# Neighbourhood attention: two heads at a time on halves of TensorE's array, with the division by the row sums on GpSimd

## The chip, the core and the metric

One core of a Trainium2 chip runs the whole program, a hybrid network of two blocks in fp32 for one sequence of 512 positions. The metric is the device time of one execution in microseconds; the time before is the median of three runs.

## What is computed

The change touches one phase, the neighbourhood attention of the second block. The 512 queries lie on a grid of 8 rows and 64 columns. There are 8 heads of width 64. Every query attends, in one softmax, to the 512 positions of the grid and to 256 context keys. The window covers all 8 rows and 16 columns around the query; outside it the logits are minus infinity, and inside it a learned bias is added. Cut to what matters:

```
s_lat = einsum('bqhd,brkhd->bhqrk', q * 64 ** -0.5, k) + bias     # -inf outside the window of columns
s_ctx = einsum('bqhd,bchd->bhqc', q * 64 ** -0.5, kc)
p = softmax(concatenate([s_lat, s_ctx], -1), -1)                  # 512 + 256 logits a query
y = einsum('bhqrk,brkhd->bqhd', p_lat, v) + einsum('bhqc,bchd->bqhd', p_ctx, vc)
```

## The kernel before, in words

The program is a list of phases (`plan`, line 234; run by `run_plan`, line 239); each phase is a block in which every engine has its own queue of instructions, and all engines meet at its end. `attention_phase` (line 1647) stands between the second block's large projection (`project_phase`, line 325, whose products are lines 402 and 406) and the phases of the gated delta rule, which begin with a clearing of the used semaphores on GpSimd (`recycle`, line 197) and two loads (line 230).

On chip a tensor lies in planes of 128 partitions by 512 fp32 columns (`pl`). Queries and keys are stored transposed: plane `h // 2` holds heads 2i and 2i+1, one on partitions 0 to 63 and one on 64 to 127. A unit of work is one head `h` and one tile `i` of 128 queries, 32 units in all, head by head. For a unit n:

- SyncE loads the bias plus mask for the tile, 128 x 512, in two loads (line 1670) into one of three buffers `B`, once the unit three before has used its own.
- TensorE makes the scores (`scores`, lines 1681 and 1682): 64 contraction rows, so half of the array's rows, 128 x 512 to one PSUM bank and 128 x 256 (context) to another; banks 0 to 3 serve two units.
- VectorE (`logits`) scales the context part (line 1720), scales and adds the bias on the grid part (line 1721), both to the buffer `Sx` (three of them), takes the row maximum (line 1723) and negates it (line 1724).
- ScalarE (`exps`, line 1747) takes the exponential in place with the negated maximum as bias, and the row sum as accumulator.
- VectorE takes the reciprocal of the sum (line 1731) and multiplies the 128 x 768 row of `Sx` by it, in place (line 1732).
- TensorE transposes six blocks of 128 x 128 (line 1708) to banks 4 and 5. It waits for the copies of the unit before.
- ScalarE copies them to `PT` in two parts, 512 columns (line 1755) and 256 (line 1756).
- TensorE multiplies the values (`values`, line 1693): six products of 128 contraction rows and 64 output partitions, so half of the array's columns, added up in bank 6 or 7 on the half of the partitions that the head has.
- ScalarE stores 64 x 128 (`store`, line 1740).

The order on each engine is written out by hand. TensorE: the scores of unit n+2, the values of n-1, the transposes of n. VectorE: reciprocal and division of n, the logits of n+2. ScalarE: the copies of n, the store of n-1, the exponential of n+2. An fp32 product stands in the profile as two instructions, each with its load of weights: 64 where the code calls 32 times. A transpose is one.

Other lines that are named below: 2341, the experts' products, which write two experts to the two column halves by turns; 1145, products on quarters of the array in an earlier phase; 2454, a GpSimd `tensor_scalar` with a per-partition scalar on 128 x 1024; 1402 and 1984, GpSimd `tensor_tensor`; 1546, a VectorE reduction; 2016, a VectorE `tensor_scalar` from and to SBUF; 2010, a VectorE operation with one input in PSUM.

## Time and profile before

| | |
|---|---|
| runs | 3935.38, 3941.82, 3942.22 us; median 3941.82 |
| profiled execution | 3941.83 us, span 3940.0 us |
| busy share of the span | TensorE 88%, its loads of weights 48%, VectorE 32%, ScalarE 15%, GpSimd 16% |
| mean granted TensorE clock | 0.935 of full speed |
| the attention phase | 2590.9 to 2722.3 us of the span |

The span is the stretch between the first and the last instruction of the profiled execution; the execution's own time is what is compared with the runs. "PE" is TensorE's products, "PEld" its loads of weights, DVE VectorE, ACT ScalarE, POOL GpSimd and SP SyncE, the queue of loads. The granted clock is a share of 2.4 GHz: 0.50 is 1.2 GHz. A duration of a TensorE instruction includes its way through the array, so successive ones overlap; the cost of one in a stream is the distance between starts. Lines such as "x12" are instructions that follow each other and are shown as one.

### The profile page before, as it was taken

To read this page: it belongs to the slowest core of one execution; us is meant where nothing else is said; L and a number is where in the kernel's file an instruction comes from. 1 tells how busy PE (TensorE), PEld (TensorE's weight loads), DVE (VectorE), ACT (ScalarE), POOL (GpSimd) and SP (SyncE) were. 2 spreads that over 40 slices of the span, in tenths; PEclk is the share of its full clock that TensorE was granted. 3 is DMA by queue.
4 is the path that set the end of the run, shared out by engine and by line. 5 is a ranking of instruction groups with operands and counts; after the bars stand their busy time and mean duration, and the time that the engine had idled before them with its cause. 6 is when DMAs were issued, how large, how long until landed. Compare 5 with 4: busy or idle time off the path is not lost. (4 is left out here: it accounts for less than half of the span.)

```text
span 3940.0 us, 43660 instructions
## 1 busy us (share of the span) xinstructions
PE 3474.0 (88%) x18392; PEld 1885.3 (48%) x18392; DVE 1252.8 (32%) x2117; ACT 580.7 (15%) x1082; POOL 613.6 (16%) x400
## 2 busy tenths in 40 slices
PE   8988999989998899879999869998678785988886
PEld 3454444743444776334444434874477753422222
DVE  1442151032123664114440142145555543101112
ACT  1032030000003331000000010034132301100001
POOL 0000020000002452009968000000131300000000
PEclk9999999998998999989999879998789896999999
DMA  3211223201320000424434112221000011399995
GB/s 143 76 33 43 70 79 101 75 28 48 106 70 1 3 3 29 139 68 124 133 120 155 51 38 75 89 68 38 1 1 1 1 44 69 135 409 409 409 409 227
DMA packets 120513, 406.22 MB, mean 103 GB/s; under 512 B 13824, under 2 KB 18560, under 8 KB 120064
## 3 DMA queue, kind: packets, MB, share of 16 engines
q1 hardware_dynamic: 113408, 378.25, 27.1%
q0 software_dynamic: 6912, 25.17, 2.0%
q8 instruction: 148, 2.42, 0.3%
q14 instruction: 45, 0.37, 0.0%
HBM read 399.17 MB, written 4.19 MB: 102 GB/s over the span
## 5 line engine op out<-in xcount | busy, mean ns | idle before, releaser
L406 PE MATMUL ps<-arena 128*128 128x512 f32 (+1 forms) x3936 | 1679.3, 589 | 88.2 <-PEq L557 22.1
L406 PEld LDWEIGHTS ps<-arena 128*128 128x128 f32 x3936 | 757.1, 193 | 1010.4 <-issue 991.9
L2341 PE MATMUL ps<-arena 128*64 128x512 f32 x1024 | 244.9, 601 | 33.0 <-DMA arena<-in_w_gate 15.5
L1936 PE MATMUL ps<-arena 128*128 128x128 f32 x1312 | 174.9, 295 | 25.9 <-POOL arena L1991 25.9
L1402 POOL TENSOR_TENSOR arena<-arena 128x512 f32<-128x512 f32 x64 | 80.2, 1269 | 751.9 <-DVE arena L1504 658.5
L455 DVE SCALAR_TENSOR_TENSOR arena<-ps,params,arena 128x511 f32<-128x511 f32 (+4 forms) x266 | 190.7, 717 | 9.5
L2454 POOL TENSOR_SCALAR arena<-arena,small 128x1024 f32<-128x1024 f32 x64 | 183.3, 2864 | 8.1 <-DMA arena<-in_w_mod 4.2
L1936 PEld LDWEIGHTS ps<-arena 128*128 128x128 f32 x1312 | 168.5, 207 | 30.2 <-issue 16.8
L449 DVE TENSOR_SCALAR arena<-ps,params 128x512 f32<-128x512 f32 x68 | 55.1, 810 | 388.2 <-PE ps L406 388.2
L2341 PEld LDWEIGHTS ps<-arena 128*64 128x64 f32 x1024 | 71.0, 136 | 201.2 <-issue 198.2
L2407 DVE SCALAR_TENSOR_TENSOR arena<-ps,mods,arena 128x512 f32<-128x512 f32 x64 | 48.1, 751 | 371.6 <-PE ps L2329 370.8
L402 PE MATMUL ps<-arena 128*128 128x128 f32 (+1 forms) x1120 | 137.4, 284 | 15.8 <-PEq L557 15.8
L402 PEld LDWEIGHTS ps<-arena 128*128 128x128 f32 x1120 | 137.6, 207 | 18.1 <-issue 18.0
L1984 POOL TENSOR_TENSOR arena<-arena,cst 128x512 f32<-128x512 f32 x24 | 26.9, 1144 | 757.9 <-ACT arena L1968 757.9
L2369 PE MATMUL ps<-arena 128*64 128x512 f32 x512 | 121.5, 617 | 21.8 <-DMA arena<-in_w_down 12.4
L435 ACT ACTIVATE arena<-arena 128x512 f32<-128x512 f32 (+2 forms) x60 | 36.1, 601 | 688.7 <-DVEq L459 688.7
L2456 POOL TENSOR_TENSOR arena<-arena 128x1024 f32<-128x1024 f32 x56 | 132.1, 2359 | 4.7
L426 ACT ACTIVATE arena<-ps 128x512 f32<-128x512 f32 (+1 forms) x75 | 43.1, 574 | 597.0 <-PE ps L406 505.7
L304 PE MATMUL ps<-arena 128*128 128x512 f32 x256 | 116.7, 607 | 6.1 <-ACT arena L313 4.2
L1153 PE MATMUL ps<-arena 64*64 64x64 f32 x3072 | 114.6, 226 | 2.5 <-ACT arena L1342 2.5
L1153 PEld LDWEIGHTS ps<-arena 64*64 64x64 f32 x3072 | 104.6, 139 | 10.2 <-issue 6.4
L1976 ACT ACTIVATE arena<-ps 128x512 f32<-128x512 f32 x132 | 78.9, 597 | 183.0 <-PE ps L1936 124.9
(387 smaller groups left out, 3350.3 us busy)
## 6 DMA issues: line engine op xcount, KB each, us to landing
arena<-in_w_in SPq DMA_DIRECT2D x166, 512.0 KB, 3.6
arena<-in_w_gate SPq DMA_DIRECT2D x128, 512.0 KB, 15.5
arena<-in_w_up SPq DMA_DIRECT2D x128, 512.0 KB, 15.6
arena<-in_w_down SPq DMA_DIRECT2D x128, 512.0 KB, 15.6
arena<-in_w_mod POOLq DMA_DIRECT2D x48, 512.0 KB, 4.1
arena<-in_ffn_up SPq DMA_DIRECT2D x44, 512.0 KB, 3.6
arena<-in_w_branch SPq DMA_DIRECT2D x32, 512.0 KB, 3.6
arena<-in_w_out SPq DMA_DIRECT2D x16, 512.0 KB, 3.6
```

The lines of the kernel that those rows point to most:

```text
L304: ins = k.nc.tensor.matmul(k.bank(self.banks[i % len(self.banks)]), w[:, q * P:(q + 1) * P], self.fills[i][1](q), start=(q == 0), stop=(q ...
L402: last = nc.tensor.matmul(out[:, t * m:(t + 1) * m], j["rhs"](ka + q)[:, t * P:(t + 1) * P], w[:, q * m:(q + 1) * m], start=(q == 0), stop ...
L406: last = nc.tensor.matmul(out[0:m, 0:j["n"]], w[:, q * m:(q + 1) * m], j["rhs"](ka + q), start=(ka + q == 0), stop=(ka + q == kt - 1))
L455: ins = nc.vector.scalar_tensor_tensor(out=o, in0=s, scalar=c, in1=o, op0=ALU.mult, op1=ALU.add)
L1153: ins = nc.tensor.matmul(k.bank(b)[half(q), cell(h, i)], l[half(q), cell(h, i)], other, start=True, stop=True)
L1402: tt = lambda o, x, y, op: nc.gpsimd.tensor_tensor(o, x, y, op)
L1936: mm = lambda l, r: nc.tensor.matmul(out, l, r, start=True, stop=True)
L1976: nc.scalar.activation(dst, k.bank(n % BANKS), ACT.Copy).then_inc(act_out, 1)
L2341: ins = nc.tensor.matmul(k.bank(b + f)[64 * e:64 * e + 64, :], xev(q, 2 * p + e), slot(g + e)[:, f * 512:f * 512 + 512], start=(q == 0), s ...
L2369: ins = nc.tensor.matmul(k.bank(6 + f)[64 * e:64 * e + 64, :], HT(u)[:, q * P + 64 * e:q * P + 64 * e + 64], slot(g + e)[:, f * 512:f * 51 ...
L2454: k.pool_chain(pool, nc.gpsimd.tensor_scalar(o, w(m), c, None, ALU.mult))
L2456: k.pool_chain(pool, nc.gpsimd.tensor_tensor(a, a, o, ALU.add))
```

## The change

Two heads of a pair, 2i and 2i+1, are worked on together for each tile: `n` now counts pairs (16), `m` single heads (32), in the order tile by tile within a pair of heads. The scores of both heads are issued together, the grid parts of the two row halves to banks 0 and 1, then the context parts to banks 2 and 3; TensorE waits with them until the logits of the pair before have been taken. The values of both heads are issued by turns to the two halves of the partitions of bank 7, and stored with one operation of 128 x 128. The transposes of a head go to bank 6 (two blocks) and to bank 4 or 5 (four blocks); a head's transposes wait until ScalarE has copied the two blocks of the head before and the four blocks of the head two before. The division is now GpSimd's. The reduction writes the negated maximum itself. `Sx` has six buffers, `PT` and `B` four; the main part of the work space and a second one change places. The order: TensorE scores n+2, transposes 2n, transposes 2n+1, values n-1; VectorE logits of pair n+1, reciprocal 2n, maxima of pair n+1, reciprocal 2n+1; ScalarE exponential m+2, copies m (256 columns first, then 512), and after an odd m the store of the pair before. The call passes a second work space.

```diff
-def attention_phase(k, q, kt, v, kc, vc, y, w):
+def attention_phase(k, q, kt, v, kc, vc, y, w, w2):
     nc = k.nc
     pl = k.pl
     NK = T + CTX
-    units = [(h, i) for h in range(8) for i in range(TT)]
-    B = lambda n: pl(w + n % 3)
-    Sx = lambda n: pl(w + 3, 5)[:, (n % 3) * NK:(n % 3) * NK + NK]
-    PT = lambda n: pl(w + 8, 3)[:, (n % 2) * NK:(n % 2) * NK + NK]
-    cols = k.small
-    b_in = [k.sem(f"a_b_in{i}") for i in range(3)]
-    s_ok, s_used, max_ok, e_ok, p_ok, t_ok, t_out, y_ok, y_out = (k.sem(f"a_{s}") for s in ("s_ok", "s_used", "max_ok", "e_ok", "p_ok", "t_ok", "t_out", "y_ok", "y_out"))
+    heads = [(2 * hp + e, i) for hp in range(4) for i in range(TT) for e in range(2)]
+    UNITS = len(heads) // 2
+    B = lambda m: pl(w + m % 4 if m % 4 < 3 else w2 + 6)
+    Sx = lambda m: pl(w + 3, 9)[:, (m % 6) * NK:(m % 6) * NK + NK]
+    PT = lambda m: pl(w2, 6)[:, (m % 4) * NK:(m % 4) * NK + NK]
+    top = lambda m: k.small[:, 2 * (m % 6):2 * (m % 6) + 1]
+    total = lambda m: k.small[:, 2 * (m % 6) + 1:2 * (m % 6) + 2]
+    lat = lambda m: k.bank(m % 2)
+    ctx = lambda m: k.bank(2 + m % 2)[:, 0:CTX]
+    four = lambda m: k.bank(4 + m % 2)
+    two = k.bank(6)[:, 0:2 * P]
+    out = k.bank(7)[:, 0:P]
+    b_in = [k.sem(f"a_b_in{i}") for i in range(4)]
+    s_ok, s_used, max_ok, e_ok, r_ok, p_ok, t_ok, two_out, four_out, y_ok, y_out = (
+        k.sem(f"a_{s}") for s in ("s_ok", "s_used", "max_ok", "e_ok", "r_ok", "p_ok", "t_ok", "two_out", "four_out", "y_ok", "y_out"))
     with nc.Block() as block:
         @block.sync
         def _(sp):
-            for n, (h, i) in enumerate(units):
-                if n >= 3:
-                    sp.wait_ge(s_used, n - 2)
+            for m, (h, i) in enumerate(heads):
+                if m >= 4:
+                    sp.wait_ge(s_used, m - 3)
                 for r in range(2):
                     row = 2 * i + r
-                    sp.dma_start(B(n)[64 * r:64 * r + 64, :], k.dram["rpb"][h, :, (7 - row) * 64:(15 - row) * 64]).then_inc(b_in[n % 3], 16)
+                    sp.dma_start(B(m)[64 * r:64 * r + 64, :], k.dram["rpb"][h, :, (7 - row) * 64:(15 - row) * 64]).then_inc(b_in[m % 4], 16)
         @block.tensor
         def _(pe):
             def scores(n):
-                h, i = units[n]
-                lo = 64 * (h % 2)
-                if n >= 2:
-                    pe.wait_ge(s_used, n - 1)
-                a, b = k.bank(2 * (n % 2)), k.bank(2 * (n % 2) + 1)[:, 0:CTX]
-                lhs = pl(q + h // 2)[lo:lo + 64, i * P:(i + 1) * P]
-                nc.tensor.matmul(a, lhs, pl(kt + h // 2)[lo:lo + 64, :], start=True, stop=True)
-                nc.tensor.matmul(b, lhs, kc[lo:lo + 64, h // 2, :], start=True, stop=True).then_inc(s_ok, 1)
+                if n >= 1:
+                    pe.wait_ge(s_used, 2 * n)
+                hp, i = heads[2 * n][0] // 2, heads[2 * n][1]
+                lhs = lambda e: pl(q + hp)[64 * e:64 * e + 64, i * P:(i + 1) * P]
+                for e in range(2):
+                    nc.tensor.matmul(lat(2 * n + e), lhs(e), pl(kt + hp)[64 * e:64 * e + 64, :], start=True, stop=True)
+                for e in range(2):
+                    ins = nc.tensor.matmul(ctx(2 * n + e), lhs(e), kc[64 * e:64 * e + 64, hp, :], start=True, stop=True)
+                ins.then_inc(s_ok, 1)
+            def turn(m):
+                pe.wait_ge(p_ok, m + 1)
+                if m >= 1:
+                    pe.wait_ge(two_out, m)
+                if m >= 2:
+                    pe.wait_ge(four_out, m - 1)
+                for j in range(6):
+                    dst = two[:, j * P:(j + 1) * P] if j < 2 else four(m)[:, (j - 2) * P:(j - 1) * P]
+                    ins = nc.tensor.transpose(dst, Sx(m)[:, j * P:(j + 1) * P], k.const("ident"))
+                ins.then_inc(t_ok, 1)
             def values(n):
-                h, i = units[n]
-                lo = 64 * (h % 2)
-                pe.wait_ge(t_out, n + 1)
-                if n >= 2:
-                    pe.wait_ge(y_out, n - 1)
-                out = k.bank(6 + n % 2)[lo:lo + 64, 0:P]
+                hp = heads[2 * n][0] // 2
+                pe.wait_ge(four_out, 2 * n + 2)
+                if n >= 1:
+                    pe.wait_ge(y_out, n)
                 for j in range(6):
-                    vv = v[:, j, h * 64:h * 64 + 64] if j < 4 else vc[:, j - 4, h * 64:h * 64 + 64]
-                    ins = nc.tensor.matmul(out, vv, PT(n)[:, j * P:(j + 1) * P], start=(j == 0), stop=(j == 5))
+                    for e in range(2):
+                        c = (2 * hp + e) * 64
+                        vv = v[:, j, c:c + 64] if j < 4 else vc[:, j - 4, c:c + 64]
+                        ins = nc.tensor.matmul(out[64 * e:64 * e + 64, :], vv, PT(2 * n + e)[:, j * P:(j + 1) * P], start=(j == 0), stop=(j == 5),
+                                               skip_group_check=True)
                 ins.then_inc(y_ok, 1)
             scores(0)
             scores(1)
-            for n in range(len(units) + 1):
-                if n + 2 < len(units):
+            for n in range(UNITS):
+                if n + 2 < UNITS:
                     scores(n + 2)
+                turn(2 * n)
+                turn(2 * n + 1)
                 if n >= 1:
                     values(n - 1)
-                if n < len(units):
-                    pe.wait_ge(p_ok, n + 1)
-                    if n >= 1:
-                        pe.wait_ge(t_out, n)
-                    for j in range(6):
-                        ins = nc.tensor.transpose(k.bank(4 + j // 4)[:, (j % 4) * P:(j % 4 + 1) * P], Sx(n)[:, j * P:(j + 1) * P], k.const("ident"))
-                    ins.then_inc(t_ok, 1)
+            values(UNITS - 1)
         @block.vector
         def _(dve):
             link = lambda ins: k.dve_chain(dve, ins)
             def logits(n):
-                dve.wait_ge(s_ok, n + 1)
-                dve.wait_ge(b_in[n % 3], 32 * (n // 3 + 1))
-                if n >= 3:
-                    dve.wait_ge(t_ok, n - 2)
-                nc.vector.tensor_scalar(Sx(n)[:, T:NK], k.bank(2 * (n % 2) + 1)[:, 0:CTX], 0.125, None, ALU.mult)
-                nc.vector.scalar_tensor_tensor(out=Sx(n)[:, 0:T], in0=k.bank(2 * (n % 2)), scalar=0.125, in1=B(n), op0=ALU.mult, op1=ALU.add).then_inc(s_used, 1)
-                dve.wait_ge(s_used, n + 1)
-                link(nc.vector.tensor_reduce(cols[:, 2 * (n % 3):2 * (n % 3) + 1], Sx(n), AX.X, ALU.max))
-                nc.vector.tensor_scalar(cols[:, 2 * (n % 3):2 * (n % 3) + 1], cols[:, 2 * (n % 3):2 * (n % 3) + 1], -1.0, None, ALU.mult).then_inc(max_ok, 1)
+                for m in (2 * n, 2 * n + 1):
+                    dve.wait_ge(s_ok, n + 1)
+                    dve.wait_ge(b_in[m % 4], 32 * (m // 4 + 1))
+                    if m >= 6:
+                        dve.wait_ge(t_ok, m - 5)
+                    nc.vector.tensor_scalar(Sx(m)[:, T:NK], ctx(m), 0.125, None, ALU.mult)
+                    nc.vector.scalar_tensor_tensor(out=Sx(m)[:, 0:T], in0=lat(m), scalar=0.125, in1=B(m), op0=ALU.mult, op1=ALU.add).then_inc(s_used, 1)
+            def tops(n):
+                for m in (2 * n, 2 * n + 1):
+                    dve.wait_ge(s_used, m + 1)
+                    nc.vector.tensor_reduce(top(m), Sx(m), AX.X, ALU.max, negate=True).then_inc(max_ok, 1)
+            def shares(m):
+                dve.wait_ge(e_ok, m + 1)
+                nc.vector.reciprocal(total(m), total(m)).then_inc(r_ok, 1)
             logits(0)
-            logits(1)
-            for n in range(len(units)):
-                dve.wait_ge(e_ok, n + 1)
-                s = cols[:, 2 * (n % 3) + 1:2 * (n % 3) + 2]
-                link(nc.vector.reciprocal(s, s))
-                nc.vector.tensor_scalar(Sx(n), Sx(n), s, None, ALU.mult).then_inc(p_ok, 1)
-                if n + 2 < len(units):
-                    logits(n + 2)
-        def store(act, n):
-            h, i = units[n]
-            lo = 64 * (h % 2)
-            act.wait_ge(y_ok, n + 1)
-            nc.scalar.activation(pl(y + h // 2)[lo:lo + 64, i * P:(i + 1) * P], k.bank(6 + n % 2)[lo:lo + 64, 0:P], ACT.Copy).then_inc(y_out, 1)
+            tops(0)
+            for n in range(UNITS):
+                if n + 1 < UNITS:
+                    logits(n + 1)
+                shares(2 * n)
+                if n + 1 < UNITS:
+                    tops(n + 1)
+                shares(2 * n + 1)
+        @block.gpsimd
+        def _(pool):
+            for m in range(2 * UNITS):
+                pool.wait_ge(r_ok, m + 1)
+                nc.gpsimd.tensor_scalar(Sx(m), Sx(m), total(m), None, ALU.mult).then_inc(p_ok, 1)
         @block.scalar
         def _(act):
-            def exps(n):
-                act.wait_ge(max_ok, n + 1)
-                c = 2 * (n % 3)
-                nc.scalar.activation(Sx(n), Sx(n), ACT.Exp, bias=cols[:, c:c + 1], accum_out=cols[:, c + 1:c + 2]).then_inc(e_ok, 1)
+            def exps(m):
+                act.wait_ge(max_ok, m + 1)
+                nc.scalar.activation(Sx(m), Sx(m), ACT.Exp, bias=top(m), accum_out=total(m)).then_inc(e_ok, 1)
+            def store(n):
+                h, i = heads[2 * n]
+                act.wait_ge(y_ok, n + 1)
+                nc.scalar.activation(pl(y + h // 2)[:, i * P:(i + 1) * P], out, ACT.Copy).then_inc(y_out, 1)
             exps(0)
             exps(1)
-            for n in range(len(units)):
-                act.wait_ge(t_ok, n + 1)
-                if n >= 2:
-                    act.wait_ge(y_ok, n - 1)
-                nc.scalar.activation(PT(n)[:, 0:512], k.bank(4), ACT.Copy)
-                nc.scalar.activation(PT(n)[:, 512:768], k.bank(5)[:, 0:256], ACT.Copy).then_inc(t_out, 1)
-                if n >= 1:
-                    store(act, n - 1)
-                if n + 2 < len(units):
-                    exps(n + 2)
-            store(act, len(units) - 1)
+            for m in range(2 * UNITS):
+                if m + 2 < 2 * UNITS:
+                    exps(m + 2)
+                act.wait_ge(t_ok, m + 1)
+                if m >= 4:
+                    act.wait_ge(y_ok, m // 2 - 1)
+                nc.scalar.activation(PT(m)[:, 0:256], two, ACT.Copy).then_inc(two_out, 1)
+                nc.scalar.activation(PT(m)[:, 256:768], four(m), ACT.Copy).then_inc(four_out, 1)
+                if m % 2 == 1 and m >= 3:
+                    store(m // 2 - 1)
+            store(UNITS - 1)
@@ program @@
-    plan(k, attention_phase, k, NQ, NKK, vt, kc, vct, Y + 4, H_PL)
+    plan(k, attention_phase, k, NQ, NKK, vt, kc, vct, Y + 4, H_PL, w)
```

## Rows read from the trace of the kernel before

**Rows 1.** Table of stretches: us; busy PE, PEld, DVE, ACT, POOL; PEclk; DMA, GB/s
```profile
2590.50:2722.50 132.00, 127.61 (x704) 87.33 (x704) 90.13 (x192) 67.05 (x162) 0.00 (x0) 0.94 0.23 65
...
2600.00:2607.00 7.00, 7.00 (x23) 4.65 (x23) 5.00 (x11) 1.78 (x4) 0.00 (x0) 0.50 0.23 61
...
2620.00:2700.00 80.00, 80.00 (x471) 55.21 (x470) 59.75 (x129) 44.79 (x109) 0.00 (x0) 1.00 0.26 72
...
3440.00:3460.00 20.00, 14.39 (x62) 4.32 (x62) 1.29 (x2) 1.08 (x2) 0.00 (x0) 1.00 1.03 409
```

**Rows 2.** Timeline, a turn of the loop: start us, us, engine, line, x count
```profile
2652.95 1.12 PE L1681 MATMUL ps<-arena 64*128 64x512 f32 x2
...
2653.91 0.59 PE L1682 MATMUL ps<-arena 64*128 64x256 f32 x2
...
2654.43 1.52 PE L1693 MATMUL ps<-arena 128*64 128x128 f32 x12
...
2654.54 0.42 DVE L1720 TENSOR_SCALAR arena<-ps 128x256 f32<-128x256 f32 x1 [0.82 <-PE ps L1682]
...
2654.88 0.68 DVE L1721 SCALAR_TENSOR_TENSOR arena<-ps,arena 128x512 f32<-128x512 f32 x1
...
2655.88 0.88 PE L1708 MATMUL ps<-cst,arena 128*128 128x128 f32 x6
...
2656.69 1.12 PE L1681 MATMUL ps<-arena 64*128 64x512 f32 x2
...
2656.80 0.60 ACT L1755 ACTIVATE arena<-ps 128x512 f32<-128x512 f32 x1 [1.52 <-PE ps L1708]
```

**Rows 3.** Groups by form in the phase: count, busy us, mean ns, idle before
```profile
L1723 DVE TENSOR_REDUCE small<-arena 128x1 f32<-128x768 f32 x32 | 30.5, 953 | 1.1
...
L1747 ACT ACTIVATE arena<-arena,small 128x768 f32<-128x768 f32 x32 | 29.8, 932 | 5.9 <-DVE small L1724 5.5
...
L1732 DVE TENSOR_SCALAR arena<-arena,small 128x768 f32<-128x768 f32 x32 | 19.8, 620 | 1.1
...
L1756 ACT ACTIVATE arena<-ps 128x256 f32<-128x256 f32 x32 | 12.1, 377 | 0.0
...
L1747 ACT ACTIVATION_READ_ACCUMULATOR arena<-arena,small 128x1 f32 x32 | 6.1, 191 | 0.0
...
L1731 DVE RECIPROCAL small<-small 128x1 f32<-128x1 f32 x32 | 4.9, 153 | 1.6 <-ACT arena L1747 1.6
```

**Rows 4.** Timeline, the phase's first scores and last store
```profile
2590.94 2.04 PE L1681 MATMUL ps<-arena 64*128 64x512 f32 x2 [0.54 <-PEq L364]
...
2722.03 0.27 ACT L1740 ACTIVATE arena<-ps 64x128 f32<-64x128 f32 x1 [1.32 <-PE ps L1693]
```

**Rows 5.** Timeline in the experts' products, column halves by turns
```profile
3429.70 4.88 PE L2341 MATMUL ps<-arena 128*64 128x512 f32 x21
...
3430.14 0.17 PEld L2341 LDWEIGHTS ps<-arena 128*64 128x64 f32 x2 [0.26 <-issue]
```

**Rows 6.** Timeline in the products on quarters of the array
```profile
1301.64 1.00 PEld L1145 LDWEIGHTS ps<-arena 64*64 64x64 f32 x31 [0.36 <-issue]
```

**Rows 7.** Groups by form on GpSimd
```profile
L2454 POOL TENSOR_SCALAR arena<-arena,small 128x1024 f32<-128x1024 f32 x64 | 183.3, 2864 | 8.1 <-DMA arena<-in_w_mod 4.2
```

**Rows 8.** Timeline, VectorE beside a busy GpSimd, two places
```profile
1344.42 3.72 POOL L1402 TENSOR_TENSOR arena<-arena 128x512 f32<-128x512 f32 x3 [3.08 <-issue]
...
1345.59 0.67 DVE L1546 TENSOR_REDUCE small<-arena 128x8 f32<-128x512 f32 x1
...
3003.31 4.60 POOL L1984 TENSOR_TENSOR arena<-arena,cst 128x512 f32<-128x512 f32 x4 [51.48 <-ACT arena L1968]
...
3003.66 1.20 DVE L2016 TENSOR_SCALAR arena<-arena 128x512 f32<-128x512 f32 x1
...
3004.78 4.51 DVE L2010 TENSOR_TENSOR arena<-ps,arena 128x512 f32<-128x512 f32 x7
```

**Rows 9.** The bias loads' line: ns of one issue, min/median/max
```profile
L1670 SPq DMA_DIRECT2D arena<-in_rpb x64: 465/586/1773, 2590.9 to 2701.0; - x64
```

## The prediction

> **What bounds the phase now.** I read the table of stretches first, since the change touches one phase of 131 us in a span of 3940. In it TensorE is busy 127.6 of 132 us, VectorE 90, ScalarE 67, GpSimd 0, and TensorE's granted clock is 1.00 in its main part and 0.50 at its start [rows 1]. Then one turn of the loop in the timeline: scores from 2652.95, values from 2654.43, transposes from 2655.88, the next scores from 2656.69. That is 1.48 + 1.45 + 0.81 = 3.74 us for a head of one tile with no gap, so TensorE sets the pace [rows 2]. The groups by form give what the others need for a head: VectorE 0.42 + 0.68 + 0.95 + 0.15 (negating the maximum, priced like the reciprocal) + 0.15 + 0.62 = 2.97 us, ScalarE 0.93 + 0.19 + 0.60 + 0.38 + 0.27 = 2.37 us [rows 2 to 4]. Both have room. The phase runs from its first scores (2590.94) to the last store (2722.03), 131.1 us [rows 4]; a shorter phase moves all that follows.
>
> **Part 1, TensorE.** An fp32 product is two instructions (x2 for one call, x12 for six) [rows 2]. A 512-column one takes a step T = 0.43 us, a 256-column one half, and each kind of work begins with a pause of about 0.18: 0.96 + 0.52 = 1.48 = 3T + 0.19 [rows 2].
> Values: two heads now write the two column halves by turns. The nearest rows are the experts' products, also column halves by turns: 21 instructions of 512 columns in 4.88 us, less 0.59 for the last, are 0.214 each, half of T, and two loads of weights go by in 0.17 us beside them [rows 5]. So the 24 instructions of two heads should cost what 12 do now, 1.45 us (with no overlap 2.90). I take 1.45.
> Scores: two heads on the two row halves. No row shows exactly this; without overlap a pair costs 2 x 1.48 = 2.96. The nearest row is the products on quarters of the array, which mix both row halves: 31 loads in 1.00 us, 0.033 each [rows 6], where a 64-column instruction alone would need T/8 = 0.054. So row halves overlap. But the order is both instructions of head 0, then both of head 1: the second of head 0 runs beside the first of head 1, and the half-length context ones follow. Laid out that is 4T + 0.18 = 1.90 us; with perfect pairing 3T + 0.18 = 1.47. I take 1.90.
> Transposes: 12 for two heads, unchanged in cost, 0.81 a head. The new wait: the two left blocks go to one PSUM bank, so the second head's transposes wait until ScalarE has copied the first head's. From the first transpose to ScalarE's copy 0.92 us (2655.88 to 2656.80) [rows 2], then the 256-column copy 0.38 [rows 3] and about 0.05 for the signal: 1.35 us from start to start, in place of 0.81. Behind that wait stand, in TensorE's queue, the values and the next scores.
> TensorE's own loop for a pair of heads: 1.35 + 0.81 + 1.45 + 1.90 = **5.51 us**, against 2 x 3.74 = 7.48.
>
> **Part 2, the others, for a pair of heads.** VectorE loses the division (0.62) and the negation (0.15): 2.20 a head, 4.4 a pair; of this the logits are some 0.34 + 0.62 a head from start to start, as the second operation starts 0.34 behind the first [rows 2] and I let the next one do alike, 1.9 a pair. ScalarE: two exponentials 2.25, copies 1.95, one store in place of two 0.27: 4.5 a pair [rows 3, 4].
> GpSimd now divides. Its nearest row is the same operation on 1024 columns, 2.86 us [rows 7]; at 768 columns proportional is 2.15, and with nothing saved 2.86. The time should go mostly with the columns, so I take 2.2, 4.4 a pair. It hides behind TensorE by itself, but lies in a chain over two pairs: end of scores, two heads' logits (0.2 + 1.9), reciprocal (0.2), two divisions (4.4 + 0.1), transposes 0.81, values 1.45, scores 1.90: 10.96 for two pairs, 5.48 each. That ties with 5.51; every 0.1 us more on GpSimd costs about 0.1 a pair. At 2.86 it is 6.1 a pair, +9 us in all.
> VectorE beside a busy GpSimd: an SBUF-to-SBUF tensor_scalar took 1.20 for 512 columns while GpSimd ran, where 768 columns take 0.62 here [rows 3, 8]. A reduction of 512 columns within a GpSimd stretch took 0.67, in proportion to the 0.95 for 768 here, and seven operations that read PSUM, most of them beside the same GpSimd stretch, took 4.51, 0.64 each [rows 3, 8]. The only operation of the first kind in this loop is the division that leaves it. So I charge VectorE nothing; the rival below has the other end.
> SP: 64 bias loads as before, one buffer more and a wait one head further ahead, two a head of 0.59 us of issue each, 1.2 against a pace of 2.75, hidden behind the loop; an issue that came late would cost its own 1.77 us at most, once [rows 9]. The clearing of a few more semaphores after the phase is on GpSimd's queue: under 1 us, taken as 0.
>
> **Part 3, start and tail.** At the start the clock is 0.50 [rows 1] and the same two score instructions take 2.04 against 1.12, 1.8 times [rows 2, 4]; I take 1.9 for the steps alone. The walk in us from the first scores: scores of pair 0 end at 3.9; logits 5.8; scores of pair 1 waited for those, end 9.7; logits 11.6; first reciprocal 11.8; divisions end 14.0, 16.2, 19.8 (the third waits for the scores and logits of pair 2) and 22.0; transposes, values of pair 0, first store at 24.5. Then 15 further stores: 13 at 5.5, one at about 4.6 (no scores left; GpSimd's 4.4 rules) and the last at about 1.7, as it waits for no further transposes: 77.8. Sum 102.3. If the low clock lasts a pair longer, 2 us more. I take 103, which is **28 us less** than 131.1. The profiled execution took 3941.83 us, the median of three runs is 3941.82, so nothing is to be shifted: 3941.8 - 28 = **3914 us**.
>
> **A rule against this.** The rows show loads of weights going by beside a running product on the same rows of the array [rows 5]. The Trainium skill (TensorE: Matmul & The Clock Gate, Part 3, the mechanism) says that a load overlaps a running matmul only when the row group differs, and the two column halves of the values share all rows; by it this sum would lose its largest gain. Its price stands under rival 3.
>
> **Rivals.**
> 1. The row halves don't overlap: scores 2.96 a pair, the loop 6.57, 13 x 1.06 + 3 at the start = +17: **3931**. For: no row of exactly this form. Against: rows 6. 11%.
> 2. VectorE's reductions and reciprocals wait for GpSimd's division to end. Reciprocal 0.15, division 2.2, two reductions 1.9 only then, reciprocal, and the next logits 1.9 beside the second division: about 6.7 a pair, +18: **3932**. For: the tensor_scalar that waited. Against: the reduction in rows 8. 8%.
> 3. The loads of the values stay exposed on the column halves: 24 x (T/4 = 0.107, and 0.033 a load from rows 6) + 0.18 = 3.5 in place of 1.45, the loop 7.6, +33: **3947**, no change. Against: rows 5. 4%.
> 4. The other side: the clock doesn't come back. The phase starts at 0.50, and TensorE would now pause 0.54 us in every pair, where the loop before had no gap. At 0.50 a pair costs TensorE (0.81 + 0.81 + 1.45 + 1.90) x 1.9 = 9.4, with the signal 9.8, against 7.48: if it stays so for all 16 pairs, +37 us on before, **3977**. A low-clock pair costs 4.3 more than a full one, the gain is 2.0 a pair, so it decides from about 7 of 16 pairs on. For: rows 1, the start. Against: the experts' stretch keeps 1.00 with TensorE busy 14.4 of 20 us [rows 1]; here it would be busy about nine tenths. 6%.
> That it doesn't do what it says is rival 1 or 3.
>
> **How the numbers follow.** The forecast, with GpSimd's step anywhere in its bounds, has 71%. Its own span: perfect pairing of the scores takes 13 x 0.43 + 1.5 = 7 us off (3907), the unscaled GpSimd step adds 9 (3923). The range for 8 in 10 takes in these, 2 us below for the start, and rivals 1 and 2: 3905 to 3932. A measurement of this kernel tells about 0.2% (8 us) from no change. Faster by more: the forecast, rival 1 and most of rival 2, 0.86. Within: rest of 2 and rival 3, 0.07. Slower: rival 4 and mishaps, 0.07.
>
> **What would show it.** The phase about 103 us long; in the timeline a pair every 5.5 us; the 24 value instructions in 1.5 us; scores 1.9 a pair; a gap of about 0.5 us between the two heads' transposes, ended by ScalarE's copy of 256 columns; GpSimd's division 2.2 us; VectorE's reduction still 0.95 and its reciprocal 0.15; granted clock 1.00 from about 20 us into the phase. Wrong would be: scores at 3 us (rival 1), a reduction over 1.5 us (2), values over 3 us (3), a clock under 0.9 over the main part (4), or the longest wait on GpSimd, which means its step is over 2.3.

## The result, and the profile after

| | before | after |
|---|---|---|
| median of the runs | 3939.7 us (3935.4 to 3942.2, four runs) | 3901.85 us (3898.8 to 3903.7, four runs) |
| ratio | | 0.9904, 95% interval 0.9887 to 0.9921 |
| profiled execution, its span | 3941.83, 3940.0 us | 3900.27, 3898.5 us |
| first scores to last store | 131.1 us | 95.35 us |
| a pair of heads in the main part | 7.49 us | 5.21 us |

The change makes the kernel 38 us faster, 1.0%. The forecast was 28 us (3914, range 3905 to 3932): right in direction, and the measured time lies 3 us below the range.

The page's row of engines; of a local change little shows here, and the one sign of it is that GpSimd has some 70 us more, which are its 32 divisions:

```profile
PE 3421.6 (88%) x18392; PEld 1849.9 (47%) x18392; DVE 1227.1 (31%) x2053; ACT 575.2 (15%) x1066; POOL 682.7 (18%) x432
```

One turn of the new loop in the timeline; it answers to [rows 2], and all lines are new ones of the new kernel: 1698 transposes, 1710 values, 1685 and 1687 scores, 1782 ScalarE's copy of the 256 columns, 1761 GpSimd's division.

```profile
2640.37 0.88 PE L1698 MATMUL ps<-cst,arena 128*128 128x128 f32 x6
...
2641.28 0.38 ACT L1782 ACTIVATE arena<-ps 128x256 f32<-128x256 f32 x1 [1.09 <-PE ps L1698]
...
2641.77 0.85 PE L1698 MATMUL ps<-cst,arena 128*128 128x128 f32 x6 [0.52 <-POOL arena L1761]
...
2642.54 1.29 PEld L1710 LDWEIGHTS ps<-arena 128*64 128x64 f32 x24 [0.17 <-issue]
2642.54 1.53 PE L1710 MATMUL ps<-arena 128*64 128x128 f32 x24
2642.60 4.38 POOL L1761 TENSOR_SCALAR arena<-arena,small 128x768 f32<-128x768 f32 x2 [0.92 <-DVE small L1745]
...
2644.01 1.13 PE L1685 MATMUL ps<-arena 64*128 64x512 f32 x4
...
2644.97 0.60 PE L1687 MATMUL ps<-arena 64*128 64x256 f32 x4
...
2645.50 0.88 PE L1698 MATMUL ps<-cst,arena 128*128 128x128 f32 x6
...
2647.04 0.87 PE L1698 MATMUL ps<-cst,arena 128*128 128x128 f32 x6 [0.67 <-POOL arena L1761]
```

From the first head's transposes (2640.37) to those of the second 1.40 us, then 0.77, the values 1.47 (2642.54 to 2644.01), the scores 1.49 (2644.01 to 2645.50): 5.13 us. The wait of 2641.77 is put down to GpSimd, whose division had ended at 2641.68 (2642.60 less 0.92 idle); ScalarE's copy ended at 2641.66, so the two tie here, and experiment 3 has the same 1.40 with no division on GpSimd at all. In the next pair the second head's transposes start at 2647.04, 1.54 behind the first's, and their wait ends with GpSimd: 5.30 us. The two kinds of pair alternate, and the mean over the 13 intervals between stores is 5.21. What the new and the moved operations cost, in the groups by form of the phase (columns as in [rows 3]):

```profile
L1761 POOL TENSOR_SCALAR arena<-arena,small 128x768 f32<-128x768 f32 x32 | 70.1, 2203 | 446.6 <-DVE small L1745 446.6
...
L1741 DVE TENSOR_REDUCE small<-arena 128x1 f32<-128x768 f32 x32 | 28.7, 939 | 0.0
...
L1745 DVE RECIPROCAL small<-small 128x1 f32<-128x1 f32 x32 | 4.9, 153 | 3.1 <-ACT arena L1767 3.1
```

GpSimd's division takes 2.20 us (forecast 2.2), VectorE's reduction 0.94 and its reciprocal 0.15, as in [rows 3], although GpSimd is busy 41.7 of 50 us. The waits of the main part, 2615 to 2670 (columns: who waited for whom, us in total, times, longest), show TensorE's transposes (1698) behind GpSimd, 6.6 us in 11 waits, ties included, where [rows 2] had no gap on TensorE:

```profile
PE ps L1698 <- POOL arena L1761: 6.6, 11, 0.7
```

The start, answering to [rows 4]. Columns as in the timeline above.

```profile
2586.40 2.08 PE L1685 MATMUL ps<-arena 64*128 64x512 f32 x4 [0.54 <-PEq L364]
```

```profile
2589.78 0.42 DVE L1735 TENSOR_SCALAR arena<-ps 128x256 f32<-128x256 f32 x1 [32.91 <-DMA arena<-in_rpb]
...
2591.99 1.13 PE L1685 MATMUL ps<-arena 64*128 64x512 f32 x4 [2.65 <-DVE arena L1736]
...
2592.95 0.80 PE L1687 MATMUL ps<-arena 64*128 64x256 f32 x4
...
2595.91 4.38 POOL L1761 TENSOR_SCALAR arena<-arena,small 128x768 f32<-128x768 f32 x2 [435.26 <-DVE small L1745]
...
2600.89 8.75 POOL L1761 TENSOR_SCALAR arena<-arena,small 128x768 f32<-128x768 f32 x4 [0.60 <-DVE small L1745]
...
2607.71 0.28 ACT L1772 ACTIVATE arena<-ps 128x128 f32<-128x128 f32 x1 [0.60 <-PE ps L1710]
```

And the third last and the last store:

```profile
2675.40 0.28 ACT L1772 ACTIVATE arena<-ps 128x128 f32<-128x128 f32 x1 [0.60 <-PE ps L1710]
...
2681.75 0.28 ACT L1772 ACTIVATE arena<-ps 128x128 f32<-128x128 f32 x1 [1.71 <-PE ps L1710]
```

First scores to first store are 21.3 us, the 13 intervals after it 67.7, the last two 4.4 and 2.0. The table of stretches (columns as in [rows 1]) has the granted clock of the start. It is at 0.50 under the first scores, at 1.00 for 3.4 us, at 0.50 again for 6.8 us, and at 1.00 for good from 2600.05, 13.7 us into the phase:

```profile
2586.80:2589.40 2.60, 2.53 (x8) 0.85 (x6) 0.00 (x0) 0.85 (x1) 0.00 (x0) 0.50 0.49 132
2589.80:2593.20 3.40, 1.21 (x8) 0.69 (x8) 3.29 (x6) 0.37 (x1) 0.00 (x0) 1.00 0.71 203
2593.80:2599.80 6.00, 4.00 (x14) 2.32 (x14) 4.82 (x11) 2.00 (x5) 3.89 (x2) 0.50 0.49 145
2600.20:2606.00 5.80, 3.88 (x26) 2.61 (x26) 5.23 (x12) 5.25 (x12) 5.20 (x4) 1.00 0.40 113
2620.00:2670.00 50.00, 44.04 (x430) 31.36 (x428) 37.37 (x79) 36.16 (x87) 41.69 (x20) 1.00 0.30 86
```

**Where the 38 us are.** The phase is 35.7 us shorter. The rest is most likely not the change's: in the thirteen profiles of this study (before, after and eleven experiments) the phase's first scores start between 2584.4 and 2592.8 us although the code ahead of it is the same in all of them, and in the pair compared here the one after started 4.5 us sooner (2586.4 against 2590.9). What follows the phase takes nearly as long as before (1217.7 and 1216.5 us). Against the 33 runs of the kernel before that stand beside the experiments below (medians 3938.0 to 3938.8 us) the 3901.9 would be 36 to 37 us less, close to the phase's 35.7. So the length of the phase is the sharper measure, and the tables below give it beside the time.

### The profile page after: what moved, and what is told of

Its sections match the earlier page's. It is cut to its first block and busy times, and to the rows that moved or that the text cites. A ratio compares the mean times of both kernels' runs of the same rounds, so it can differ in the third digit from the quotient of the medians.

```text
span 3898.5 us, 43598 instructions
## 1 busy us (share of the span) xinstructions
PE 3421.6 (88%) x18392; PEld 1849.9 (47%) x18392; DVE 1227.1 (31%) x2053; ACT 575.2 (15%) x1066; POOL 682.7 (18%) x432
## 5 line engine op out<-in xcount | busy, mean ns | idle before, releaser
L1959 PE MATMUL ps<-arena 128*128 128x128 f32 x1312 | 177.7, 298 | 21.1 <-POOL arena L2014 20.5
L1761 POOL TENSOR_SCALAR arena<-arena,small 128x768 f32<-128x768 f32 x32 | 70.1, 2203 | 446.6 <-DVE small L1745 446.6
```

The source lines that it names most:

```text
L1959: mm = lambda l, r: nc.tensor.matmul(out, l, r, start=True, stop=True)
```

## The experiments

| kernel | time, us | phase, us | a pair, us | to first store, us |
|---|---|---|---|---|
| before | 3939.7 | 131.1 | 7.49 | 17.9 |
| after | 3901.9 | 95.4 | 5.21 | 21.3 |
| 1: both heads on one row half | 3935.7 | 129.7 | 6.41 | 35.8 |
| 1: both heads on one column half | 3920.4 | 114.4 | 6.43 | 23.2 |
| 2: scores issued head by head | 3899.6 | 97.8 | 5.22 | 23.7 |
| 2: values issued head by head | 3916.7 | 108.0 | 6.05 | 22.7 |
| 3: after, VectorE divides | 3899.1 | 91.8 | 5.12 | 20.7 |
| 3: before, GpSimd divides | 3939.7 | 132.0 | 7.49 | 18.8 |
| 4: values between the transposes | 3896.6 | 86.9 | 4.56 | 21.4 |
| 4: reciprocals first | 3899.5 | 92.6 | 5.12 | 20.8 |
| 4: both orders | 3892.3 | 85.1 | 4.56 | 20.5 |
| 4: values between, VectorE divides | 3897.2 | 91.2 | 5.03 | 20.9 |
| 5: both orders, start filled | 3891.5 | 83.7 | 4.56 | 19.3 |

A pair is the interval between two stores in the main part at the full clock. The phase ends with two or three shorter intervals, as no scores are left for them.

The runs of the kernel before beside these had medians of 3938.0 (experiments 1 and 3), 3938.5 (2, and the first two of 4) and 3938.8 us (the rest). The phase and the pair are of one profile of each kernel. The intervals of a main part repeat to 0.02 us (those of after alternate, 5.13 and 5.30); the start is less sure, as the fall of the clock in the scores by head shows (experiment 2). The times alone separate the new kernel from the three that take overlap away (3914.2 us and more), and its runs (3898.8 to 3903.7) from those with the values between the transposes (3894.0 to 3897.2) and with both orders (3888.9 to 3895.6; 3891.2 to 3893.0 with the start filled), though these were run at other times; between the other variants of after their runs overlap, and what is said of them rests on the profiles.

### 1. What each pair of halves is worth

Both heads' scores from the same row half (`e1_rows_same`; head 1's queries and keys are left out, so that its output is another one, while the sizes of all operations stay):

```diff
-                    nc.tensor.matmul(lat(2 * n + e), lhs(e), pl(kt + hp)[64 * e:64 * e + 64, :], start=True, stop=True)
+                    nc.tensor.matmul(lat(2 * n + e), lhs(0), pl(kt + hp)[0:64, :], start=True, stop=True)
...
-                    ins = nc.tensor.matmul(ctx(2 * n + e), lhs(e), kc[64 * e:64 * e + 64, hp, :], start=True, stop=True)
+                    ins = nc.tensor.matmul(ctx(2 * n + e), lhs(0), kc[0:64, hp, :], start=True, stop=True)
```

> Both heads' scores are made from partitions 0 to 63 (head 0's queries and keys twice), so the row halves can't overlap; head 1's output is head 0's scores with head 1's values. Theory (TensorE's loop of two transposes with the wait between them, values, scores sets the pace): scores go from 1.48 to 2.96 us a pair, the loop from 5.2 to 6.6, 13 x 1.4 plus 3 at the start, so the phase goes from 95.4 to about 117 us and the time from 3902 to about 3923. Rival (the chain through GpSimd over two pairs sets the pace, and TensorE has room): a pair costs half of the 1.48 more, the phase about 107, the time about 3913.

Measured: 3935.7 us, ratio to before 0.9993 (0.9983 to 1.0002). The timeline of its main part:

```profile
2647.05 1.98 PE L1685 MATMUL ps<-arena 64*128 64x512 f32 x4
...
2649.83 0.88 PE L1698 MATMUL ps<-cst,arena 128*128 128x128 f32 x6
```

Scores 1.83 + 0.95 = 2.78 us against 1.49: the row halves overlap fully in the new kernel and save 1.3 us a pair. The pair is 6.41, 1.2 over the new kernel's 5.21, so nearly all of the longer scores comes through to the pair. But the phase lost 34 us and not the 22 expected. The stretches show why:

```profile
2587.00:2634.00 47.00, 41.31 (x124) 23.94 (x124) 18.87 (x38) 14.06 (x30) 17.07 (x8) 0.50 0.28 79
2634.40:2660.00 25.60, 23.52 (x177) 15.89 (x178) 15.05 (x32) 14.79 (x37) 14.75 (x8) 1.00 0.26 72
```

and, for comparison, the kernel before:

```profile
2591.00:2607.00 16.00, 15.44 (x36) 8.88 (x37) 10.43 (x22) 5.03 (x9) 0.00 (x0) 0.50 0.39 108
```

The clock stays at 0.50 until 2634.4, 47.6 us into the phase, with TensorE busy 41.3 of 47 us; the new kernel has 0.50 for some 10 us in all, the kernel before for 17. It isn't this one profile alone: the mean granted clock is 0.931 to 0.933 in all ten runs of this kernel, and 0.934 to 0.938 in the 19 runs of the kernel before beside them. The first store comes 14.5 us later and the second one 11.7 behind it, 6.5 over the new kernel's pair; the other 13 of the 34 us are 11 pairs of 1.2. So the longer scores cost some 15 to 18 us and the low clock the rest, up to 20.

Both heads' values to the same column half (`e2_cols_same`):

```diff
-    out = k.bank(7)[:, 0:P]
+    outs = lambda e: k.bank(7)[0:64, e * P:(e + 1) * P]
...
-                        ins = nc.tensor.matmul(out[64 * e:64 * e + 64, :], vv, PT(2 * n + e)[:, j * P:(j + 1) * P], start=(j == 0), stop=(j == 5),
+                        ins = nc.tensor.matmul(outs(e), vv, PT(2 * n + e)[:, j * P:(j + 1) * P], start=(j == 0 and e == 0), stop=(j == 5),
...
-                nc.scalar.activation(pl(y + h // 2)[:, i * P:(i + 1) * P], out, ACT.Copy).then_inc(y_out, 1)
+                nc.scalar.activation(pl(y + h // 2)[0:64, i * P:(i + 1) * P], outs(0), ACT.Copy)
+                nc.scalar.activation(pl(y + h // 2)[64:128, i * P:(i + 1) * P], outs(1), ACT.Copy).then_inc(y_out, 1)
```

> Both heads' values are written to partitions 0 to 63 (two column ranges of the same bank), so the column halves can't overlap, and the store is two operations of 64 x 128. Theory (TensorE's loop sets the pace): values from 1.45 to 2.9 us a pair, the loop from 5.2 to 6.6, the phase about 115, the time about 3921. Rival (GpSimd's chain sets the pace): half of it, the phase about 105, the time about 3912. If the loads of weights had been the limit of the values and not the overlap of the products, nothing would change: 3902.

Measured: 3920.4 us, phase 114.4, both as the theory had it.

```profile
2644.66 2.83 PE L1710 MATMUL ps<-arena 128*64 128x128 f32 x24
2647.42 1.13 PE L1685 MATMUL ps<-arena 64*128 64x512 f32 x4
```

The same 24 instructions take 2.76 us against 1.47. Each pair of halves is thus worth 1.2 to 1.3 us a pair, of the 2.3 that a pair became shorter; with both gone the pair would be some 5.2 + 1.2 + 1.2 = 7.6, about the old 7.49 (an estimate; it wasn't run).

### 2. Does the order of issue make the overlap?

The forecast had TensorE start its instructions in the order of the queue, and so the scores at 4T + 0.18 = 1.90 us; measured are 1.49, which is 3T + 0.2. The timeline of after can be narrowed to the start of these instructions. Between 2644.00 and 2644.02 it shows two of them at work:

```profile
2644.01 0.70 PE L1685 MATMUL ps<-arena 64*128 64x512 f32 x2
```

and half a microsecond later, between 2645.0 and 2645.1, the other two:

```profile
2644.54 0.60 PE L1685 MATMUL ps<-arena 64*128 64x512 f32 x2
```

Four such instructions on the same rows took 1.83 us in experiment 1, so I read this as the two heads starting together, 0.53 ahead of their second instructions, although both instructions of head 0 stand in front of head 1's first. Scores issued head by head (`e5_scores_by_head`):

```diff
                 for e in range(2):
                     nc.tensor.matmul(lat(2 * n + e), lhs(e), pl(kt + hp)[64 * e:64 * e + 64, :], start=True, stop=True)
-                for e in range(2):
                     ins = nc.tensor.matmul(ctx(2 * n + e), lhs(e), kc[64 * e:64 * e + 64, hp, :], start=True, stop=True)
```

> The scores are issued head by head: grid and context part of head 0, then those of head 1. Theory (each tile of the array starts its own instructions, whatever stands between them in the queue): the two heads still start together, scores stay at 1.48 us a pair, time about 3902. Rival (instructions start in the order of the queue, and the pairing seen comes from the order of issue): head 1 starts about when head 0's last context part does, scores about 2.5 to 2.9 us a pair, the loop about 6.3, phase about 112, time about 3918.

Measured: 3899.6 us; scores from 2644.44 to 2645.94, 1.50 us, and the pairs as in the new kernel. Narrowed to 2644.43 to 2644.46, the timeline shows two 512-column instructions under way from 2644.44 on, 0.71 us together. (One alone lasts 0.69 in experiment 1.) The one beside head 0's first must be head 1's first, and three instructions of head 0 stand between the two in the queue:

```profile
2644.44 0.71 PE L1685 MATMUL ps<-arena 64*128 64x512 f32 x2
```

The whole group:

```profile
2644.44 1.14 PE L1685 MATMUL ps<-arena 64*128 64x512 f32 x4
...
2645.94 0.87 PE L1697 MATMUL ps<-cst,arena 128*128 128x128 f32 x6
```

Its phase is 2.5 us longer, nearly all of it before the first store, where the clock fell to 0.50 once more for 3.4 us (2604.5 to 2607.9); the main part is the same. The values issued head by head (`e6_values_by_head`):

```diff
-                for j in range(6):
-                    for e in range(2):
+                for e in range(2):
+                    for j in range(6):
```

> The values are issued head by head: twelve instructions of head 0, then twelve of head 1. Theory (tiles start on their own): still 1.45 us a pair, 3902. Rival (order of the queue): 2.8 to 2.9 us a pair, the loop 6.5, phase about 114, time about 3920. In between would show how far ahead TensorE looks.

Measured: 3916.7 us, phase 108.0.

```profile
2644.05 2.45 PE L1710 MATMUL ps<-arena 128*64 128x128 f32 x24
2646.43 1.13 PE L1685 MATMUL ps<-arena 64*128 64x512 f32 x4
```

2.38 us for the 24, between 1.47 and the 2.76 of one column half: 0.38 of 1.29 us of the overlap is left. The trace has the place of it. Up to 2644.979 nine of the 24 have started, 0.11 us apart, the ninth at 2644.975; a view that ends at 2644.985 has the tenth too, which starts at 2644.981:

```profile
2644.05 1.20 PE L1710 MATMUL ps<-arena 128*64 128x128 f32 x9
```

```profile
2644.05 1.25 PE L1710 MATMUL ps<-arena 128*64 128x128 f32 x10
```

From there two rows of starts, each 0.11 us apart, run side by side for four instructions, until the first has had twelve; the rest of the second goes on alone. So I read the tenth start as head 1's first, beside head 0's ninth, with head 0's last three between them in the queue. It is the same in every pair of the phase, and three is also what head 1 stepped over in the scores by head. An instruction can thus start ahead of three of the other half of the array; that more than three are never stepped over is what twelve in a row suggests, and no other number was tried.

### 3. Is GpSimd's division worth anything?

The new kernel with the division back on VectorE (`e3_divide_on_vector`):

```diff
-                nc.vector.reciprocal(total(m), total(m)).then_inc(r_ok, 1)
+                link(nc.vector.reciprocal(total(m), total(m)))
+                nc.vector.tensor_scalar(Sx(m), Sx(m), total(m), None, ALU.mult).then_inc(p_ok, 1)
```

> The new kernel with the division back on VectorE behind the reciprocal, GpSimd idle. Theory: VectorE needs 4.4 + 2 x 0.62 + waits = 5.7 to 5.9 us a pair and becomes the bound: 13 x 0.6 = +8, phase about 103, time about 3910. Rival (GpSimd's 2.2 us a head is the bound now, its removal frees more than VectorE loses): the pair goes to TensorE's 5.1, time about 3900.

Measured: 3899.1 us, phase 91.8, and so the rival's side: the phase is 3.6 us shorter than with GpSimd. VectorE is nearly at its limit (columns as in [rows 1]), but its operations follow each other closer than their durations add up, so that a turn fits into 5.12 us (and into 5.03 in experiment 4) where the durations are 4.4 + 2 x 0.62 = 5.6:

```profile
2620.00:2670.00 50.00, 44.80 (x436) 31.95 (x434) 49.29 (x100) 37.78 (x89) 0.00 (x0) 1.00 0.33 93
```

and TensorE's loop runs at its own 5.12, with the second head's transposes always 1.40 behind the first's:

```profile
2640.99 0.88 PE L1698 MATMUL ps<-cst,arena 128*128 128x128 f32 x6
...
2642.39 0.85 PE L1698 MATMUL ps<-cst,arena 128*128 128x128 f32 x6 [0.52 <-issue]
...
2646.11 0.87 PE L1698 MATMUL ps<-cst,arena 128*128 128x128 f32 x6
```

Of the 3.6 us some 1.1 are these pairs (0.09 each), 0.6 the start, and 1.9 the last pairs: 1.2 in the thirteenth interval, which experiment 4 takes off as well by an earlier reciprocal with GpSimd still dividing, and 0.7 in the one behind it, where GpSimd's 4.4 us a pair lie bare. In time the two kernels can't be told apart (3895.0 to 3901.6 here, 3898.8 to 3903.7 with GpSimd).

The kernel before with GpSimd's division alone (`e4_before_pool_divides`):

```diff
-                link(nc.vector.reciprocal(s, s))
-                nc.vector.tensor_scalar(Sx(n), Sx(n), s, None, ALU.mult).then_inc(p_ok, 1)
+                nc.vector.reciprocal(s, s).then_inc(r_ok, 1)
...
+        @block.gpsimd
+        def _(pool):
+            for n in range(len(units)):
+                pool.wait_ge(r_ok, n + 1)
+                nc.gpsimd.tensor_scalar(Sx(n), Sx(n), cols[:, 2 * (n % 3) + 1:2 * (n % 3) + 2], None, ALU.mult).then_inc(p_ok, 1)
```

> The kernel before with one part of the change alone: GpSimd divides. Theory: TensorE stays the bound at 3.74 us a head; the division ended 2.2 us before the transposes that need it, and is 1.6 us longer plus a signal, so it stays hidden: 3940, within 3. Rival (VectorE's load was part of the bound): faster by more than 5 us. Other rival (the longer way through GpSimd shows): each head 0.3 us or more longer, slower by 10 us or more.

Measured: 3939.7 us, ratio 1.0004 (0.9994 to 1.0013): nothing, as expected.

```profile
2651.71 2.20 POOL L1740 TENSOR_SCALAR arena<-arena,small 128x768 f32<-128x768 f32 x1 [1.54 <-DVE small L1732]
...
2654.44 0.88 PE L1709 MATMUL ps<-cst,arena 128*128 128x128 f32 x6
```

The division that starts at 2651.71 ends at 2653.91, and the transposes start at 2654.44, still without a wait.

The moved division is therefore worth nothing in the old kernel and costs the new one, as it stands, 3.6 us of phase; the gain comes from the two pairs of halves.

### 4. What bounds the new loop, and a faster order

Two theories were open: TensorE's own loop with its wait for the copy, or GpSimd's chain over two pairs. Values between the two heads' transposes (`e7_values_between`):

```diff
                 turn(2 * n)
-                turn(2 * n + 1)
                 if n >= 1:
                     values(n - 1)
+                turn(2 * n + 1)
```

> TensorE's order is transposes of head 0, values of the pair before, transposes of head 1, so that the wait for the copy of the two blocks lies behind the values. Theory (TensorE's loop with that wait bounds): the loop falls from 5.2 to 4.6, where GpSimd's 4.4 and ScalarE's 4.5 come close; 13 x 0.6 = 8 us less, phase 87, time about 3894. Rival (GpSimd's chain over two pairs bounds already): under 2 us less, 3900 or more.

Measured: 3896.6 us (ratio to the kernel before 0.9892, 0.9875 to 0.9908), phase 86.9, a pair 4.55.

```profile
2640.07 0.87 PE L1698 MATMUL ps<-cst,arena 128*128 128x128 f32 x6
...
2640.87 1.53 PE L1710 MATMUL ps<-arena 128*64 128x128 f32 x24
...
2642.30 4.39 POOL L1761 TENSOR_SCALAR arena<-arena,small 128x768 f32<-128x768 f32 x2 [0.18 <-DVE small L1745]
...
2642.33 0.87 PE L1698 MATMUL ps<-cst,arena 128*128 128x128 f32 x6
...
2644.63 0.87 PE L1698 MATMUL ps<-cst,arena 128*128 128x128 f32 x6
```

A turn is now 4.56 (2640.07 to 2644.63) with no gap on TensorE, and the divisions follow each other on GpSimd almost without one. Reciprocals first (`e8_reciprocal_first`):

```diff
+                shares(2 * n)
                 if n + 1 < UNITS:
                     logits(n + 1)
-                shares(2 * n)
+                shares(2 * n + 1)
                 if n + 1 < UNITS:
                     tops(n + 1)
-                shares(2 * n + 1)
```

> VectorE takes the first reciprocal before the logits and the second one before the maxima, so that GpSimd never waits for the logits. Theory (TensorE's loop of 5.13 bounds and GpSimd's chain only adds the 0.08 that the mean pair is above it): 1 to 2 us less in the pairs, phase 93 to 95, time about 3900. Rival (GpSimd's chain bounds): the pair falls to 4.8 or less, phase 90, time about 3896.

Measured: 3899.5 us, phase 92.6. All pairs are now 5.12, and the 5.30 of every second one is gone, as in experiment 3. So TensorE's loop, with its wait for the copy, sets 5.13 of the 5.21, and GpSimd's chain adds 0.18 in every second pair. The phase is 2.8 us shorter than after's and 0.8 longer than with VectorE's division: most of what the move costs the new kernel is the place of the reciprocals in VectorE's queue. Both of these diffs together (`e9_both_orders`):

> Both orders together: values between the transposes of the two heads, reciprocals before logits and maxima. TensorE's loop is then 4.55 us a pair, GpSimd's two divisions 4.4, ScalarE 4.5. Theory (values between takes the loop down to 4.55 and GpSimd's own 4.4 is near): 4.5 us a pair and 1 us less at the end, phase 85 to 86, time 3895 or a little under. Rival (the orders add up, as each freed its own chain): 4.3 or less is excluded by GpSimd's 4.4, so phase under 83 would refute the reading of the bounds.

Measured: 3892.3 us (ratio to the kernel before 0.9886, 0.9871 to 0.9901), phase 85.1. The pair is the 4.56 of the values between the transposes; the reciprocals' place takes 0.8 us off the start and 1.2 off the end. TensorE is busy 45.0 of 45 us in the main part, GpSimd 43.4:

```profile
2620.00:2665.00 45.00, 45.00 (x436) 32.01 (x432) 38.75 (x80) 36.95 (x89) 43.39 (x20) 1.00 0.38 107
```

The values between the transposes, and the division on VectorE as in the first diff of experiment 3 (`e10_between_vector`):

> Values between the transposes, and the division back on VectorE. Theory (the move of the division to GpSimd is worth nothing as long as TensorE's wait bounds, and pays once it is hidden): VectorE's 4.95 us a pair bounds, phase 89 to 91, 3 to 4 us behind the same order with the division on GpSimd (86.9), time about 3899. Rival (GpSimd's longer way costs more than VectorE's load): phase under 86.9.

Measured: 3897.2 us, phase 91.2; against the same order with GpSimd (86.9) it is 4.3 us longer. The times (3896.0 to 3900.9, and 3894.0 to 3897.2 with GpSimd) overlap; the pairs, 5.03 against 4.56 twelve times over, don't.

```profile
2620.00:2665.00 45.00, 41.42 (x397) 29.02 (x394) 44.36 (x90) 33.38 (x82) 0.00 (x0) 1.00 0.34 95
```

Now VectorE bounds, busy 44.4 of 45 us with its 5.03 a pair. This is the frame in which the moved division pays: once the wait behind the transposes is hidden.

### 5. The clock at the start

Both orders, and three spare products in TensorE's pauses behind the first scores (`e11_filled_start`; their results are used by nobody):

```diff
+            spare = lambda: nc.tensor.matmul(k.bank(5), k.const("ident"), pl(kt), start=True, stop=True)
             scores(0)
+            spare()
+            spare()
             scores(1)
+            spare()
```

> Both orders, and three spare products of 128 x 512 (their result unused) in TensorE's pauses behind the first two score groups, to see whether the clock at the start depends on TensorE's pauses there. Theory (the clock comes back sooner when TensorE has work): the first store comes 2 to 4 us sooner after the first scores than the 21 us so far, phase 82 to 84. Rival (the low clock of the start lasts as long whatever TensorE does, or the spare products stand in the way): no change or 1 to 3 us longer.

Measured: 3891.5 us, phase 83.7: 1.4 us shorter than without them, the first store 1.3 us sooner (2 to 4 against the new kernel's 21.3 had been expected). The clock, with the spare products and then without them (`e9_both_orders`):

```profile
2592.20:2606.00 13.80, 10.82 (x66) 5.66 (x67) 12.50 (x25) 7.44 (x17) 9.16 (x5) 1.00 0.57 161
```

```profile
2599.80:2605.80 6.00, 3.96 (x15) 1.66 (x11) 4.64 (x12) 2.37 (x6) 5.28 (x3) 0.50 0.57 156
```

With them it is at 1.00 from 2592.1 on, 3.3 us behind the first scores (2588.9), and stays there. Both orders without them had 1.00 from 3.1 us behind theirs (2592.8) as well, but 0.50 once more from 2599.3 to 2606.1. All nine profiles with the two heads on two row halves and no spare products have this second fall of 6.8 us, and the one with them hasn't; ahead of the second and third scores TensorE waited 0.8 and 1.4 us there, against 2.6 and 2.0. So the spare products are the likely cause, on one profile with them; in time the two kernels (3892.3 and 3891.5) can't be told apart.

## Why the prediction was right or wrong

**Right.** TensorE bounds the phase before, and all but 0.18 us of every second pair after. The values cost 1.47 us a pair (taken as 1.45), GpSimd's division 2.20 (2.2), the wait between the two heads' transposes 1.40 from start to start (1.35), ended by the copy of 256 columns. VectorE paid nothing for a busy GpSimd. The bias loads stayed hidden, but for 0.4 us at the start, where VectorE's first logits (2589.78) waited for one behind the first scores (2589.34); the kernel before had a like wait. The last two stores took 6.35 us (6.3). The clock was at 1.00 for good before 20 us.

**Wrong, and by how much.** The forecast for the phase was 103 us, measured were 95.35. Three terms of the sum make the 7.7; the first is the step of the working that failed:
- Scores, "both instructions of head 0, then both of head 1 ... Laid out that is 4T + 0.18 = 1.90 us": 1.49. It took a strict order of starts from the order of issue; the starts in experiment 2 show the heads together. The scores are 0.41 us shorter than laid out and TensorE's loop 0.38 (5.51 to 5.13), and GpSimd's chain took a part of that back: it is 10.96 - 0.41 = 10.55 for two pairs by the forecast's own working, against 2 x 5.13, and 10.43 was measured. So the pair fell from 5.50 to 5.21, 13 x 0.29 = 3.8 us. The perfect pairing stood in the text as a bound of the range, and the other end was taken.
- The start, "first store at 24.5": 21.3, 3.2 us less. The first scores took 2.9 us where 3.9 were laid out; the shorter scores are in this too, and 3.9 is more than the forecast's own 1.90 x 1.9 = 3.6. And the clock was not at 0.50 all through, as the walk had it: the second scores took 1.8 us (2591.99 to 2593.75) with the clock at 1.00 up to 2593.2. The second pair's divisions ended at 18.9 (2600.89 and half of 8.75 on), not 22.0.
- 103 was taken for a sum of 102.3: 0.7.

The remaining 4 us of the difference between 3914 and 3902 are not in the phase: with a fourth run the median of before is 2 us lower (3939.7), and the other 2 are of the size of the scatter ahead of the phase, which began 4.5 us sooner in the profile of after. The range had the perfect pairing (3907) and 2 us for the start, and no term for that scatter. So the wrong step moved the forecast by 4 to 5 us (an estimate: 3.8 in the pairs and its share of the start), and it took the start and the scatter besides to leave the range by 3.

**The rivals.** 1 (rows don't overlap) is refuted by the scores' 1.49, against 2.78 on one row half in experiment 1. 2 (VectorE waits for GpSimd) by the reduction's 0.94. 3 (exposed loads) by the values' 1.47: the Trainium skill's sentence that a load overlaps a running product only with another row group (TensorE: Matmul & The Clock Gate, Part 3) would have given 3.5 here; 24 loads on the same rows went by beside the running products (2642.54, 1.29 us) and the 24 products took 1.47 in all, and the measurement decides. 4 (the clock; 3941.8 + 37 is 3979, where the forecast has 3977) did not happen in the new kernel, but experiment 1 shows that a long low clock can: with the row halves gone, it lasted 47.6 us.

The 4T rested on a strict order of starts. The Trainium skill has the same rule (TensorE: Matmul & The Clock Gate, Part 3, the mechanism: products start and end in the order of the program, without reordering). The two starts together at 2644.01 and the two at 2644.54, with head 0's second instruction issued between them, don't agree with it for heads on different row halves, and nor does head 1's start beside head 0's ninth of twelve for column halves.

**The part that the forecast didn't ask about.** It costed the moved division on GpSimd, and never asked what the two-head loop would take without the move. The answer is 3.6 us of phase less, since 2.2 us a head lie in the chain over two pairs that the forecast had found, and at the end of the phase; with the reciprocals first 0.8 of it is left.

## What to carry to other kernels

Two products of half contraction or half output width put on the two halves of the array cost what one does here, for row halves (1.49 us) and for column halves (1.47); issue the two heads' instructions by turns or in short groups, since the overlap held with four instructions of a head in a row and shrank with twelve. After such a gain look at once for the wait that has become the largest (here a copy out of the one PSUM bank between two groups of transposes) and put other work of the same queue into it: that reordering was worth 8 us of phase and 5 of time, more than moving an operation to an idle engine, which paid only afterwards (4 us of phase, not clear in the time).

## What was not expected of the hardware

- Instructions on different halves of the array start together although others stand between them in the queue: three for the row halves (1.50 us against 1.49). With twelve of a head in a row on the column halves, 30% of the overlap is left (2.38 us against 1.47 and 2.76): head 1's first starts beside head 0's ninth, again with three between.
- The low clock at the start lasted 47.6 us with both heads on one row half, and 10 us in two parts with one on each, for instructions of the same sizes in the same order. The longer scores also change TensorE's pauses there, and the two weren't separated, so the cause stays open.
- VectorE's operations without a wait between them follow each other some 0.1 us closer than their durations say: the reductions x2 of 0.94 each show as 1.80, and a turn of 5.6 us of durations takes 5.03.
